# First loads in another order, residuals in pairs and an eight-slot ring for the query projections, in a fused two-model block

## What is computed

```python
for i in range(2):                       # first block
    mod = (silu(c) @ w_mod[i] + b_mod[i]).reshape(-1, 3, 3, 1024)
    x = x + 0.5 * mod[:, 0, 2] * swiglu(modulate(x, ...), gate, up, down)
    x = x + mod[:, 1, 2] * (ssd_mixer if i == 0 else mla_mixer)(modulate(x, ...))
    x = x + 0.5 * mod[:, 2, 2] * swiglu(modulate(x, ...), gate, up, down)
for l in range(2):                       # second block
    x = x + gate1 * (rwkv7 and pooling mix of modulate(x, ...))
    x = x + gate2 * peer_ffn(modulate(x, ...))   # 8 heads, top 16 of 128*128 experts
out = rmsnorm(x) * lnf
```

## Time and profile before

| | us |
|---|---|
| median of three runs | 3544.99 (3544.09 to 3548.17) |
| the profiled execution | 3544.45 |
| its span, first to last instruction | 3542.7 |
| PE busy in it | 3363.8 |
| DVE busy | 2582.7 |
| ACT busy | 1609.1 |
| transfers, mean | 200 GB/s |

### The profile page before, as it was taken

One profiled execution on the slowest core, in us unless ns is written; L12 is line 12 of the kernel. 1 busy time (PEld: TensorE's weight loads), 2 busy tenths in 40 slices (PEclk: granted clock), 3 DMA queues, 4 the chain that ended last, 5 costly groups with the idle time before them and its releaser, 6 DMA issues.

```text
span 3542.7 us, 68786 instructions
## 1 busy us (share of the span) xinstructions
PE 3363.8 (95%) x26804; PEld 3227.9 (91%) x26804; DVE 2582.7 (73%) x4576; ACT 1609.1 (45%) x2583; POOL 198.8 (6%) x331
## 2 busy tenths in 40 slices
PE   6999989999999998999999989999899999999998
PEld 5999869999867998889999989998789999989998
DVE  7879667788736886746977757776845978767776
ACT  3456644354445435234454444444414444444444
POOL 1100001101000220200000000000300000000000
PEclk9999999999999999999999999999999999999999
DMA  9954218869622993035664466665214665456665
GB/s 366 358 196 170 78 48 326 311 254 335 215 78 107 394 354 125 31 105 190 233 205 168 164 203 228 227 227 173 72 57 158 232 222 173 166 180 228 229 227 174
DMA packets 246577, 707.44 MB, mean 200 GB/s; under 512 B 27472, under 2 KB 93008, under 8 KB 244928
## 3 DMA queue, kind: packets, MB, share of 16 engines
q1 hardware_dynamic: 212112, 571.64, 46.3%
q0 software_dynamic: 34224, 132.46, 10.0%
HBM read 669.40 MB, written 34.60 MB: 199 GB/s over the span
## 4 chain that ended last, share of the span: by engine, by line
PE 83%; DVE 7%; DMA 5%; ACT 3%; issue 2%; SPq 0%; ACTq 0%; DVEq 0%; POOLq 0%; POOL 0%
PE psum L506 37%; PE psum L539 27%; PE psum L1061 3%; DMA ring<-stream 3%; PE psum L883 2%; PE psum L996 1%; PE psum L634 1%; DMA arena<-mod_weights 1%; DVE ring L1613 1%; PE psum L903 1%; DVE arena L1544 1%; PE psum L518 1%; PE psum L519 1%; ACT weights_hi L1126 1%; DVE arena L1670 1%
## 5 line engine op out<-in xcount | busy, mean ns | idle before, releaser
L1126 ACT ACTIVATE weights_hi<-ring 128x1024 fp32r<-128x1024 f32 x727 | 769.0, 1058 | 1068.3 <-DMA ring<-stream 1017.7
L1613 DVE TENSOR_TENSOR ring<-ring,weights_hi 128x1024 fp32r<-128x1024 f32 x727 | 890.0, 1226 | 477.6 <-ACT weights_hi L1126 474.5
L506 PE MATMUL psum<-hh,weights_hi 128*128 128x256 f32 x4216 | 1210.6, 287 | 20.0 <-ACT arena L1339 8.5
L506 PE MATMUL psum<-h,weights_hi 128*128 128x256 f32 x4216 | 1196.6, 284 | 0.0
L506 PE MATMUL psum<-hh,ring 128*128 128x256 f32 x3104 | 881.5, 284 | 0.0
L506 PEld LDWEIGHTS psum<-hh,weights_hi 128*128 128x128 f32 x4216 | 813.1, 193 | 27.0 <-issue 11.9
L539 PE MATMUL psum<-small,weights_hi 128*128 128x256 f32 x2752 | 783.4, 285 | 39.9 <-DVE work L1648 21.6
L506 PEld LDWEIGHTS psum<-h,weights_hi 128*128 128x128 f32 x4216 | 812.9, 193 | 0.2
L539 PE MATMUL psum<-work,weights_hi 128*128 128x256 f32 x2752 | 781.6, 284 | 0.0
L539 PE MATMUL psum<-small,ring 128*128 128x256 f32 x2304 | 651.3, 283 | 0.0
L506 PEld LDWEIGHTS psum<-hh,ring 128*128 128x128 f32 x3104 | 598.0, 193 | 0.0
(11 more groups left out here) (409 smaller groups left out, 3904.7 us busy)
## 6 DMA issues: line engine op xcount, KB each, us to landing
ring<-stream SPq DMA_DIRECT2D x751, 512.0 KB, 3.5
arena<-mod_weights POOLq DMA_DIRECT2D x224, 512.0 KB, 5.9
arena<-stream SPq DMA_DIRECT2D x206, 512.0 KB, 5.5
acts<-small SPq DMA_DIRECT2D x256, 128.0 KB, 2.2
work<-acts SPq DMA_DIRECT2D x256, 128.0 KB, 2.1
arena<-cond_rows POOLq DMA_DIRECT2D x3, 1024.0 KB, 9.0
arena<-w_uq POOLq DMA_DIRECT2D x1, 3072.0 KB, 10.4
arena<-constants POOLq DMA_DIRECT2D x2, 1200.0 KB, 5.7
```

The costliest lines, as they stand in the source:

```text
L506: mm = pe.matmul(out, lhs[:, d, :], rhs[:, d, :], start=(d == 0 and p == 0), stop=(d == DT - 1 and p == 2))
L1126: act.activation(whi[:, NTH[n] % WS, :], raw(n), ACT.Copy).then_inc(sem["block_hi"], 1)
L1613: dve.tensor_tensor(low(n), raw(n), whi[:, NTH[n] % WS, :].bitcast(F32), ALU.subtract)\
```

## The change

- The order of SP's first loads: x, the constants and the columns come behind the first six blocks, not ahead of all. The condition is loaded by its first half only, and its silu, which ACT takes for that half only, no longer waits for these loads; nor do DVE's products. The instruction on k_a moves behind them. The first modulation loads of POOL wait for eight scaled tiles instead of twelve used blocks.
- In stage 0 the first two low parts are made behind the root, the third behind the scaling.
- `norm_squares` begins with a root of one column, so the table of that function is loaded ahead of the squares.
- `rows_in_parts` signals `acc_done` behind tiles 1, 3 and 5 of the last block, and `residual` waits for these in the stages of `BY_ROWS`. For this the last turn of the value loop is written out behind it.
- In the query projections the cycle has eight slots instead of four; the vectors' blocks go back to four.
- The output leaves in four pieces of two tiles.
- The positions signal `mla_w`, and DVE's angles wait for all four loads of it.

```diff
+def query_cycle(l):
+    first = (BASE["peer_q", l] - BASE["mix_in", 0]) % RING
+    return (*((first + k) % RING for k in range(RING)), *SSD_CYCLE[RING:])
...
-          BASE["mix_in", 0]: (0, range(RING))}
+          BASE["mix_in", 0]: (0, range(RING)), **{BASE["peer_q", l]: (0, query_cycle(l)) for l in range(2)},
+          **{BASE["uv", l]: (query_cycle(l)[0], range(RING)) for l in range(2)}}
...
+ARENA_FREE = {**{BASE["ffn", f] + RING - 1: 8 * s for f, s in ((1, 2), (3, 5))},
+              **{BASE["peer_q", l] + RING: 8 * (7 + 2 * l) for l in range(2)}}
...
+BY_ROWS = (0, 2, 3, 5, 7, 9)
...
-            sp.dma_start(cols[:, :], cols_d).then_inc(sem["loads"], 16)
-            sp.dma_start(x[:, :, :], x_d).then_inc(sem["loads"], 16)
-            sp.dma_start(kept[:, :], consts_d[:, 0:KEPT]).then_inc(sem["loads"], 16)
             for n in range(NBLOCKS):
+                if n == 6:
+                    sp.dma_start(x[:, :, :], x_d).then_inc(sem["loads"], 16)
+                    sp.dma_start(kept[:, :], consts_d[:, 0:KEPT]).then_inc(sem["loads"], 16)
+                    sp.dma_start(cols[:, :], cols_d).then_inc(sem["loads"], 16)
...
-            sp.wait_ge(sem["out_ready"], DT)
-            sp.dma_start(out_d, h[:, :, :]).then_inc(sem["out_done"], 16)
-            sp.wait_ge(sem["out_done"], 16)
+            for d in range(0, DT, 2):
+                sp.wait_ge(sem["out_ready"], d + 2)
+                sp.dma_start(out_d[:, d:d + 2, :], h[:, d:d + 2, :]).then_inc(sem["out_done"], 16)
+            sp.wait_ge(sem["out_done"], 16 * DT // 2)
...
                 for d in range(DT):
                     for lhs, rhs in ((w, hi), (w, lo), (wl, hi)):
                         mm = pe.matmul(acc[:, d, :], lhs[:, d, :], rhs, start=False, stop=False, skip_group_check=True)
+                    if last and d in (1, 3, 5):
+                        mm.then_inc(sem["acc_done"], 1)
...
-                pe.wait_ge(sem["mla_w"], 48)
+                pe.wait_ge(sem["mla_w"], 64)
...
-                with pe.Fori(0, NK // 4) as i:
+                with pe.Fori(0, NK // 4 - 1) as i:
                     for k in range(4):
+                        value(k, i)
+                for k in range(4):
+                    value(k, NK // 4 - 1, k == 3)
...
             def norm_squares(s):
+                act.activation(eps[:, 6 + s:7 + s], eps[:, 0:1], ACT.Sqrt)
...
-                for n in range(2):
+                for n in range(2 if f else 1):
...
+            silu_of_cond(0)
             act.wait_ge(sem["inits"], 4)
             act.wait_ge(sem["loads"], 48)
-            silu_of_cond(0)
...
                 dve.wait_ge(sem["block_used"], 16)
+                dve.wait_ge(sem["inits"], 4)
+                dve.wait_ge(sem["loads"], 48)
                 mod_columns(0, gate=False)
+                link(dve.tensor_scalar(omk[:, :], col("k_a", 0, 8), -1.0, 1.0, ALU.mult, ALU.add))
...
                 refine(rs[:, :], rv[:, :], SQ[:, 0, :])
+                if s == 0:
+                    for p in range(2):
+                        split_lo(FIRST[0] + p)
...
-                    ready(last(d | 1))
+                    if s in BY_ROWS and d < 6:
+                        dve.wait_ge(sem["acc_done"], 3 * BY_ROWS.index(s) + d // 2 + 1)
+                    else:
+                        ready(last(d | 1))
...
-                dve.wait_ge(sem["mla_pos"], 16)
+                dve.wait_ge(sem["mla_w"], 64)
...
-                    pool.wait_ge(sem["block_used"], 12)
+                    pool.wait_ge(sem["norm_scaled"], 8)
...
-            pool.dma_start(flat(COND), cond_d[0:1, :].to_broadcast([P, 2 * D])).then_inc(sem["cond_rows"], 16)
+            pool.dma_start(COND[:, 0, :], cond_d[0:1, 0:D].to_broadcast([P, D])).then_inc(sem["cond_rows"], 16)
```

More of the change, by code:

```diff
@@ L290, in build @@
         zeros = sb("zeros", [P, P], BF16)
[L291 removed]
+        eps = sb("eps", [P, 20])
         modc = sb("modc", [P, NSUB, 24])
@@ L1065, in peer, with value @@
                 open_acc()
[L1066 removed]
+                def value(k, i, last=False):
+                    w, wl = parts(v0 + k, i)
+                    pe.wait_ge(sem["gate_lo"], i * 4 + (GATES["uv", l] + k + 1))
+                    rows_in_parts(w, wl, gat_hi[:, k, :], gat_lo[:, k, :], last)
+                with pe.Fori(0, NK // 4 - 1) as i:
                     for k in range(4):
[L1068 to L1070 removed]
+                        value(k, i)
+                for k in range(4):
+                    value(k, NK // 4 - 1, k == 3)
             def begin(s):
@@ L1594, in normed @@
                 if s in IN_PARTS:
-                    if s and s not in EARLY:
+                    if s not in EARLY:
                         split_lo(FIRST[s] + 2)
@@ L2105, in peer @@
                 residual(7 + 2 * l, lambda d: BASE["uv", l] + 2 * NK - 1)
-            dve.wait_ge(sem["inits"], 4)
-            dve.wait_ge(sem["loads"], 48)
-            link(dve.tensor_scalar(omk[:, :], col("k_a", 0, 8), -1.0, 1.0, ALU.mult, ALU.add))
             first_products()
             for s in range(NSUB):
-                if s == 0:
-                    for p in range(3):
-                        split_lo(FIRST[0] + p)
                 normed(s)
```

15 lines of the change are left out of this document (5 added, 10 removed).

## The result

| | before | after |
|---|---|---|
| median, us | 3544.54 (four runs) | 3515.96 (four runs) |
| lowest and highest | 3543.79, 3548.17 | 3511.0, 3525.37 |
| ratio of the medians, 95% interval | | 0.9921 (0.9902 to 0.9940) |
| the profiled execution, its span | 3544.45, 3542.7 | 3511.0, 3509.3 |

The changed kernel is 28.6 us faster where 15 were forecast, and its median lies 7 us under the range. The profiled execution of after is its fastest. It is 33.4 us ahead at its end, and this table says where PE is ahead by how much (before's start of that piece of work less after's, both from the traces).

A forecast was written before the change was run, and what follows sets the result against it. TensorE (PE) was taken as the bound, 83% of the chain. Terms 3.8 + 3.0 + 0.5 + 1.5 + 1.4 + 7.6 - 3.1 = 14.7 us less gave 3530.0 us, with 3523 to 3537 for 8 in 10.

The forecast's parts named there:

- The step that failed: Inside layers: matmuls keep 0.12 us each and PE runs back to back behind each place, so the shifts add up.
- Start: Stage 0: products start sooner, bound by transfers, with product 15 at 28.6; PE's first projection comes 3.8 us earlier.
- Joints: Between sublayers: pairs and early table load give 1.0 us each behind stages 0, 2, 5; stages 4 and 7 together 0.5.
- End and output: Program end: the sum directly follows PE's last matmul, 1.5 us less; output in four pieces, 1.4 us less.
- Query ring: Both query projections: block 4's waits go, two evacuation waits shrink to about 0.5 each, the clock stays up; 7.6 us less.
- Stage 4: Angles wait for all four loads: PE's hole 1.5 us longer plus a clock fall of 1.6, 3.1 us more.
- Loop tails: Last four value blocks written out behind the loop on PE, twice: taken as 0, at most 4.4 us for each.
- the rivals: Start gives nothing (0.10), query stall is transfer (0.08), stage 4 costs nothing (0.10), table drains (0.04), slower by tail fetching (0.03).

The follow-up runs named there:

- the edit alone: The kernel before with only the small constant tile eps widened from 6 to 20 columns, moving the gated values by 64 bytes: 0.9966 of before, 12 us less.
- its removal: The changed kernel with eps 6 columns wide again and the early root's 16 cells in a tile allocated last: 0.9965 of before.
- the old slots: The changed kernel with query blocks and vectors in their former slots, without SP's wait for the residual: 0.9961 of before, 10.6 us above the changed kernel.
- three variants of the kernel before: The kernel before with row operands moved: eps widened (0.9966), the high part alone 64 bytes on (0.9951), both parts 128 bytes on (0.9964).
- the rolled loop: The changed kernel with PE's value loops of 32 turns again and residuals behind stages 7 and 9 waiting for the whole block: 0.9944 of before.
- Two repairs: The changed kernel with opening matmuls ahead of the split-block waits (alone 0.9927) and stage 4's angles waiting for positions only (alone 0.9932): together 0.9908 of before.

## Why the prediction was wrong, point by point
- **The step that failed** is the sentence that inside a layer the matmuls follow at 0.12 us each and "behind each place PE runs back to back again", with which every matmul outside the joints was costed at its old time. The row was right; what was not asked is whether the change touches what sets it. It moved the moving operand of 8256 row matmuls by 64 bytes and they became 1.1 to 1.6% faster: 12 us, as the edit alone and its removal both show. That is the term that the sum lacked. The line was in the change and was left out of the sum.
- **Start**, forecast 3.8, measured 2.0 (PE's first projection begins at 43.71 to 44.90 in five profiles with the old start, at 42.08 to 44.22 in ten with the new one; medians 1.5 apart). Two terms were off by about 1.3 and 0.5. The row was read as a total of bytes by a rate; but the blocks are needed one by one, and those behind x came late, after which DVE at 1.28 each had no slack (product 15 at 29.91 for 28.6). The opening matmuls took 5.47 instead of 5.0; with eleven of sixteen at half clock that is less than the "some 7" that the prediction gave for all sixteen.
- **Joints**, forecast 1.0 each. The joint behind stage 0 gave 1.07, as forecast. The rest of the 2.4 in the table is the down projection, 1.37 shorter: 528 matmuls at 1.3 ns less are 0.7, and the clock came back at 178.5, 4.3 us into it, not at the 181.1 of the earlier trace rows, 5.0 into it, which is 0.3 more. The mechanism was read wrongly in one point: the gain is the pairs' alone, and the table's early load takes 0.46 of it. On ACT the load began 0.02 behind the instruction before it and the next followed 0.02 behind. The Trainium skill's 1.38 of drain (page "ScalarE: Activation LUTs", section "What ACT_TABLE_LOAD costs") is not seen beside its 1.28, which the trace has; taking the load out of that place didn't help the time either.
- **End and output**, forecast 1.5 and 1.4: from the start of PE's last matmul (3526.23, 3495.92) to the root it is 3.77 instead of 5.31, and from the root to the end of the span 9.6 instead of 11.2. Right.
- **Query ring**, forecast 7.6: 2.7 and 5.0 in the two layers, from PE's first query matmul to its first vector matmul, and 10.6 (with an uncertainty of some 6) by the old slots. The evacuation stays as 0.9 in two places, forecast twice 0.5. Right.
- **Stage 4**, forecast -3.1, measured -2.3 between the two profiles: the stage is 2.0 longer, and the joint behind it gave 0.25 of its own (start of the update to root, 4.98 and 4.73). The pause grew by 1.12 (forecast 1.5), and 21 matmuls in 3.80 are 1.3 more than at full clock (forecast 1.6). The fall was forecast as the change's doing, and it isn't: three variants of the kernel before have it too. That these two profiles bear the term out is luck.
- **Loop tails**, forecast 0: no hole behind the loops; and the rolled loop isn't faster.
- **The range** held only cases of the listed mechanisms, and none of the rivals was a change of the matmuls' pace. With the old address the changed kernel measures 12.4 less than before, inside the 8 to 22 of the range.

## What to carry to other kernels
A changed size of any tile moves all tiles allocated behind it. If PE is the bound, list the addresses of the matmuls' moving operands of both versions before costing anything else, and treat a shift as a term of its own with both signs. When tuning such a kernel, try a few pads of 32 to 128 bytes ahead of those tiles early: here one pad ahead of x gave 19.5 to 27 us where all the hand-made reordering gave 12.4, and any comparison of two versions is only about their code if these addresses agree. Of a gap on PE that is closed by pulling idle-time work forward, count a part only: here PE began 4.5 us sooner, the clock was at half for the next 6.0, and 2.6 of the 4.5 went back. And take a second profile of each kernel before explaining a line of 2 us.

## What the runs showed that was not expected
- The pace of back-to-back 128x128 by 128x256 fp32 matmuls, at a clock of 1.00, was 0.1200 or 0.1172 to 0.1187 with no other edit than one of the moving operand's start address. PE had no wait in these stretches, and the other engines only did more blocks in the same time. In stage 3 with h moved it went lower in two kernels (984 matmuls in 111.53, 0.1133) and not in a third with the same addresses (115.90). What decides between these is open.
- A pause of 3.34 on PE was followed by full clock in one kernel and pauses of 3.13 to 3.25 by a clock of 0.56 to 0.58 in three others; behind one of 2.30 the clock fell after 1.1 us. The length of the last pause doesn't tell the clock by itself.
- Two repairs (1.2 to 3.3, and 0.3 to 2.9, by the profile that each is set beside) didn't show in medians with intervals of 9 us. Such steps are read from several traces, or tried together.
